# Seven half-width products for 13 of the 16 column pairs of an input projection, with modulation pages, expert rows and scores moved

## The chip, the cores and the metric

One core of one Trainium2 chip runs the whole program in one launch. The metric is the device time in microseconds (us); lower is better. The core has TensorE (PE) for matrix products, VectorE (DVE), ScalarE (ACT), GpSimd (POOL) and SyncE (SP) for the rest and for issuing transfers, and 16 DMA engines that move weights from DRAM into on-chip memory. TensorE writes its results to eight PSUM banks. All data is float32.

## The reference

One inference step of two layers for T = 264 tokens: 256 of a prompt and 8 single new tokens of 8 samples with 256 cached positions each. The model width is 1024.

```python
mod = silu(c) @ w_ada + b_ada                 # six vectors of 1024 for each sequence
h = rms_norm(x, g_mix) * (1 + sc1) + sh1
q, k, v, u, g = split(h @ w_in)               # columns 512 | 512 | 512 | 512 | 2 x 1024
q, k = rms_norm(q), rms_norm(k)               # over heads of 64
o = rms_norm(softmax differences of q k over v)   # samples read cached keys and values
y = pooled windows (2/4/8/16) of u, times w_pool
x += gt1 * ((g0 * (o @ w_branch_a) + g1 * (y @ w_branch_b)) @ w_out)
h2 = rms_norm(x, g_ffn) * (1 + sc2) + sh2
x += gt2 * f(h2)    # layer 0: dense SwiGLU of 2816; layer 1: the best 2 of 8 SwiGLU experts of 3584
```

## The kernel before

Activations are kept transposed: hT holds 1024 features as 8 groups of 128 partitions, with the 264 tokens along the row. Weights come as pages through a ring of 18 slots, which SyncE fills in the order of the list `stream`: before page n it waits until the page that held its slot has been used (`pages_used`). Two column chunks of 128 make one page of 1 MB ("pair").

The input projection makes 32 column chunks. The first 16 of them (pairs 0 to 7: queries, keys, pool input u, values; `Z_ORDER`) are those of the change; 16 more are the gates. Chunk i is the sum of 8 matrix products of 128x128 weights with 264 columns (`z`, L1560); each is two instructions of TensorE. The banks 2 to 5 take turns, VectorE copies the result out (`read_z`, L2308). For each of the 8 query and key chunks ScalarE squares it, TensorE sums the squares (L1651), ScalarE takes the root and VectorE normalises it (`norm_qk`: a reciprocal at L2317, a product at L2321 or L2324). The whole order of instructions on each engine is written out by hand, with semaphores between engines.

In layer 0, four modulation pages (`later_ada`) follow each second chunk: 32 instructions of TensorE at L1470 for the four, and VectorE reads a finished group of 16 with a transposition (`read_mod`, L2091). Sample queries are transposed by TensorE, copied by VectorE (`read_sample_queries`, L2329, behind chunk 10), stored to DRAM (`q_rows`) by GpSimd and loaded back spread over all partitions. `past_scores(b)` then multiplies them with two pages of cached keys of sample b and reduces (L2345, L2348), once for each of the 8 samples; those of samples 0 and 1 stand behind chunks 14 and 15, the others behind the loop, ahead of the prompt's scores (`scores`). TensorE's products for these scores are L1578; the second of them waits for VectorE's copy at L2419, which stands behind sample 6.

The output projection and the feed-forward part of layer 0 already form two chunks at a time from seven half-size products (helper `product`, L1199), with sums of weights on VectorE (L2125 and others) and reads from PSUM with an addition (L2172). A half-size product has 132 columns.

Ahead of layer 0's projection TensorE makes bias rows for the relative positions (L1529); VectorE copies them out (L2300, L2302). Behind layer 1's attention the norm (`norm(3)`: ScalarE copies tokens at L889 and adds the shift at L893) leads to the router and to 16 turns of expert work: gate and up products (L1885) from pages `w_exp_gate` and `w_exp_up`, down products (L1906) from rows of `w_exp_down`, all issued by SyncE (L690, L705). The down rows of a turn are issued in the next turn's loop, between its gate and up pages.

## Time and profile before

| | |
|---|---|
| median of 3 runs | 1605.14 us (1605.09 to 1605.17) |
| profiled execution | 1605.13 us, span 1603.2 us |
| TensorE busy | 1565.8 us (98% of the span) |
| VectorE busy | 541.9 us (34%) |
| ScalarE busy | 181.6 us (11%) |
| GpSimd busy | 69.6 us (4%) |
| DMA | 535.30 MB, mean 334 GB/s |
| layer 0's projection, first 16 chunks | 33.99 to 114.5 us |
| layer 1's projection, first 16 chunks | 484.1 to 545.6 us |
| experts | 702 to 1591 us |

The profile is one execution. Busy times of engines overlap. What an engine waits for is read from semaphores. The span ends with the last instruction; the profiled execution's own time is 1.9 us longer than it.

### The profile page before, as it was taken

The numbers are of one execution on the slowest core, as the hardware profiler recorded it, in microseconds if no ns is written. First come the engines' busy times: TensorE is split into PE (matmuls) and PEld (weight loads), VectorE is DVE, ScalarE is ACT, GpSimd is POOL, SyncE is SP. The second block draws the span as 40 slices with busy tenths as digits, with TensorE's granted clock in tenths as the row PEclk, the third lists the DMA queues.
The fourth block names the chain that finished last, engine by engine and source line by source line (L and its number), as shares of the span: only waits on it lengthen the run. The fifth ranks groups of instructions, "written<-read, shape, count | busy, mean of one in ns | idle before, by whom it ended". The sixth has DMA issues, their size and how long they took to land.

```text
span 1603.2 us, 37188 instructions
## 1 busy us (share of the span) xinstructions
PE 1565.8 (98%) x16734; PEld 1003.9 (63%) x16734; DVE 541.9 (34%) x1182; ACT 181.6 (11%) x486; POOL 69.6 (4%) x118
## 2 busy tenths in 40 slices
PE   7999999999999999999999999999999999999997
PEld 3777898999998878944444444444554555555554
DVE  4368378666554783741101100110011011101132
ACT  2102313111112032131000000000000000000000
POOL 1112400000000110010000000000000000000010
PEclk9999999999999999999999999999999999999999
DMA  9999869666359755569999999999999999999995
GB/s 361 364 386 369 281 219 329 229 223 215 128 174 311 245 165 171 171 237 383 418 418 404 418 418 403 419 418 404 419 402 417 417 398 418 410 406 417 408 378 183
DMA packets 174340, 535.30 MB, mean 334 GB/s; under 512 B 12535, under 2 KB 101413, under 8 KB 161378
## 3 DMA queue, kind: packets, MB, share of 16 engines
q1 hardware_dynamic: 158706, 497.20, 80.9%
q0 software_dynamic: 8768, 28.96, 5.2%
q10 hardware_dynamic: 6704, 6.72, 1.3%
q8 instruction: 134, 2.20, 0.6%
q14 instruction: 28, 0.23, 0.0%
HBM read 517.47 MB, written 15.82 MB: 333 GB/s over the span
## 4 chain that ended last, share of the span: by engine, by line
PE 85%; DMA 11%; DVE 3%; issue 1%; ACT 1%; SPq 0%; DVEq 0%
PE banks L1885 30%; PE banks L1560 14%; PE banks L1199 14%; PE banks L1906 14%; DMA ring<-in_w_exp_up 10%; PE banks L1470 2%; PE banks L1740 2%; PE banks L1231 1%; DVE inv L2504 1%; PE banks L1727 1%; PE banks L1578 1%; DMA ring<-in_w_ada 1%; PE banks L1651 0%; DMA ring<-in_w_exp_down 0%; ACT hT L893 0%
## 5 line engine op out<-in xcount | busy, mean ns | idle before, releaser
L1885 PE MATMUL banks<-ring,area 128*32 128x448 f32 x3072 | 302.6, 539 | 3.3 <-DMA ring<-in_w_exp_up 2.7
L1885 PE MATMUL banks<-ring,xT 128*32 128x448 f32 x3072 | 301.8, 539 | 3.1 <-DMA ring<-in_w_exp_up 3.1
L1560 PE MATMUL banks<-hT,ring 128*128 128x264 f32 x1024 | 239.6, 389 | 3.8 <-ACT hT L893 3.7
L576 DVE TENSOR_TENSOR area<-banks,area 128x448 f32<-128x448 f32 x48 | 46.4, 966 | 576.4 <-ACT area L1157 576.4
L1906 PE MATMUL banks<-area 128*32 128x256 f32 x3840 | 227.4, 379 | 1.4 <-issue 1.1
L1560 PEld LDWEIGHTS banks<-hT,ring 128*128 128x128 f32 x1024 | 193.1, 191 | 39.3 <-issue 6.8
L1885 PEld LDWEIGHTS banks<-ring,area 128*32 128x32 f32 x3072 | 109.8, 110 | 164.5 <-issue 157.4
L1885 PEld LDWEIGHTS banks<-ring,xT 128*32 128x32 f32 x3072 | 111.7, 110 | 160.8 <-issue 151.5
L1906 PEld LDWEIGHTS banks<-area 128*32 128x32 f32 x3840 | 138.8, 110 | 100.6 <-issue 44.2
L1157 ACT ACTIVATE area<-banks 128x448 f32<-128x448 f32 x48 | 26.1, 543 | 779.3 <-PE banks L1885 779.3
L1906 PE MATMUL banks<-ring,area 128*32 128x256 f32 x1536 | 89.4, 379 | 2.0 <-DMA ring<-in_w_exp_down 1.4
L1906 PEld LDWEIGHTS banks<-ring,area 128*32 128x32 f32 x1536 | 55.5, 110 | 39.4 <-issue 13.4
L1199 PE MATMUL banks<-area,ring 128*128 128x132 f32 x480 | 58.4, 277 | 2.3 <-DVE area L2570 1.9
L1199 PEld LDWEIGHTS banks<-area,ring 128*128 128x128 f32 x480 | 56.0, 190 | 3.2 <-DVE area L2570 2.6
L1470 PE MATMUL banks<-ring,cT 128*32 128x256 f32 x768 | 50.1, 397 | 0.8 <-DMA ring<-in_w_ada 0.8
L1199 PE MATMUL banks<-sq,ring 128*128 128x132 f32 x352 | 46.8, 276 | 0.0
L1199 PE MATMUL banks<-area 128*128 128x132 f32 x392 | 45.7, 276 | 0.0
L1199 PEld LDWEIGHTS banks<-area 128*128 128x128 f32 x392 | 44.9, 190 | 0.0
L1199 PE MATMUL banks<-sq,area 128*128 128x132 f32 x352 | 43.3, 276 | 0.1
L1199 PEld LDWEIGHTS banks<-sq,ring 128*128 128x128 f32 x352 | 43.0, 190 | 0.0
L1199 PEld LDWEIGHTS banks<-sq,area 128*128 128x128 f32 x352 | 41.3, 190 | 0.3 <-issue 0.3
L845 POOL DMA_INDIRECT hT<-y_rows,row_of x2 | 2.0, 976 | 813.6 <-ACTq L1165 813.3
(362 smaller groups left out, 1252.7 us busy)
## 6 DMA issues: line engine op xcount, KB each, us to landing
ring<-in_w_exp_gate SPq DMA_DIRECT2D x128, 896.0 KB, 17.6
ring<-in_w_exp_up SPq DMA_DIRECT2D x128, 896.0 KB, 19.7
area<-in_w_exp_down SPq DMA_DIRECT2D x64, 1024.0 KB, 18.1
ring<-in_w_ada SPq DMA_DIRECT2D x96, 512.0 KB, 8.6
ring<-in_w_in SPq DMA_DIRECT2D x32, 1024.0 KB, 13.6
ring<-in_w_exp_down SPq DMA_DIRECT2D x32, 1024.0 KB
...
ring<-in_w_ff_gate SPq DMA_DIRECT2D x11, 1024.0 KB, 6.4
```

The costliest lines, as they stand in the source:

```text
L576: dve.tensor_tensor(F["act_tok"][:, t, :].rearrange("p (i n) -> p n i", i=BODY), bank[3 + t][:, 0:SLICE].rearrange("p (n i) -> p n i", i=B ...
L1157: act.activation(FFN["silu_tok"][:, t, :], bank[t][:, 0:SLICE], ACT.Silu).then_inc(s.silu_e, 1)
L1199: mm = pe.matmul(out, w[c], x[c], start=(first and c == 0), stop=(last and c == n - 1), skip_group_check=True)
L1231: mm = pe.matmul(left(u), w[:, c, 0:P], hT[:, c, 0:HALF], start=(c == 0), stop=(c == 3), skip_group_check=True)
L1470: mm = pe.matmul(bank[b][32 * g:32 * g + 32, half * S:(half + 1) * S].rearrange("p (c n) -> p c n", c=DC), cT[:, r, :], w[:, :, 32 * g:32 ...
L1560: mm = pe.matmul(bank[b][:, 0:T], w[:, c, :], hT[:, c, :], start=(c == 0), stop=(c == DC - 1))
L1578: mm = pe.matmul(bank[4 + 2 * (n % 2) + m][:, 0:w], ATT["q_n"][r, h, i * P:(i + 1) * P], ATT["kT"][r, h, 0:w], start=True, stop=True)
L1727: mm = pe.matmul(bank[2 + j % 2][:, 0:T], branch[j][:, H + c, :], ATT["yT"][:, c, :], start=(c == 0), stop=(c == H - 1))
L1740: mm = pe.matmul(bank[4 + j % 2][:, 0:T], branch[j][:, c, :], oT[:, c, :], start=(c == 0), stop=(c == H - 1))
L1885: mm = pe.matmul(bank[t + 3 * half][32 * g:32 * g + 32, 0:SLICE], tokens[:, t, 32 * r:32 * r + 32], w[half][:, SLICE * g:SLICE * (g + 1)], ...
L1906: mm = pe.matmul(bank[6 + t // 2][32 * q:32 * q + 32, (t % 2) * S:(t % 2 + 1) * S], FFN["actT"][:, m % 2, t, 32 * i:32 * i + 32], wide(at) ...
L2504: step(dve.reciprocal(inv[:, :], root[:, h % 2, :]))
```

## The change

1. **Halved pairs.** For pairs 1 to 7 of layer 0 and 1 to 6 of layer 1 (`Z_HALVED`) the 2x2 blocks of the weights (two chunks by two halves of the 1024 features) and of hT (two halves of features by two halves of the tokens) are combined in seven products of four 128x128 matrix products with 132 columns, in place of eight such products. VectorE makes four sums of weights for each pair (`sum_z`, 128x512 elements each, the last in the page itself) and four sums of hT once for each layer (`sum_h_z`). ScalarE copies products 1, 6 and 5 out of PSUM (`z_one`, `z_two_five`), VectorE adds the others to them (`z11`, `z12`, `z22`) and copies the last (`z21`). Pairs that aren't halved are made as before (`z_whole`), with two banks a pair.
2. **Modulation pages.** Of layer 0's pages 16 to 47, only 16 to 31 stay in its projection. Pages 32 to 39 are streamed between the branch and the output weights and multiplied right ahead of the output projection, 40 to 47 in feed-forward pairs 2 to 5 (`last_ada`). One read of 16 pages becomes two of 8.
3. **Order on VectorE.** `past_scores(0)` and `(1)` follow the projection loop. The sample queries are copied in pair 6, the sample keys in pair 7, modulation in pair 5, the old pool state in pairs 2 and 3.
4. **Bias rows.** ScalarE copies them out, ahead of the projection loop, in place of VectorE.
5. **Unread products.** In layer 0, six products of 256 columns (`WARM`) that nobody reads stand between the last bias row and the first projection product. They need nothing that isn't already there.
6. **Expert rows.** Five down rows of the first turn (`EARLY_ROWS`, 2 + 2 + 1) are issued by ScalarE in `norm(3)`, ahead of its copies of tokens, and SyncE leaves them out later.

```diff
--- before.py
+++ after.py
+WARM = 6
+Z_UNITS = 8
+Z_HALVED = (1, 2, 3, 4, 5, 6, 7), (1, 2, 3, 4, 5, 6)
...
-        STATE_AT = (5, 7)
+        STATE_AT = (2, 3)
...
+        EARLY_ROWS = ((2, 2), (4, 2), (6, 1))
...
-            return range(16 + 2 * (i - 1), min(16 + 2 * (i + 1), 48)) if l == 0 and i % 2 else range(0)
+            return range(16 + 2 * (i - 1), min(16 + 2 * (i + 1), 32)) if l == 0 and i % 2 else range(0)
...
+        def last_ada(i):
+
+            return range(36 + 2 * i, 38 + 2 * i) if 2 <= i <= 5 else range(0)
...
+                    for n in range(32, 40) if (kind, l, j) == ("out", 0, 0) else ():
+                        yield ada_page(0, n)
...
+                    for n in last_ada(j // 2):
+                        yield ada_page(0, n)
...
+        Z_LEFT, Z_RIGHT = (2, 4), (3, 5)
...
-                elif at < RING:
+                else:
                     sp.wait_ge(s.pages_used, STRAIGHT)
-                else:
-                    sp.wait_ge(s.x_new, 3 * DC)
-                    sp.wait_ge(s.pooled, LAYERS)
...
-                            down_rows_in(m - 1, i, n)
+                            if m > 1 or (i, n) not in EARLY_ROWS:
+                                down_rows_in(m - 1, i, n)
...
+                    for i, n_rows in EARLY_ROWS:
+                        at = eslot[2 * DC + i]
+                        act.dma_start(run(at, n_rows), A["w_exp_down"][0, 0, 0:WIDE, :].rearrange(
+                            "(p i) d -> p (i d)", i=BODY)[:, i * D:(i + n_rows) * D]).then_inc(page_in[at], 16)
...
+                def z_one(u):
+                    act.wait_ge(s.product_mm, z_finished(l, 1, u))
+                    act.copy(z_chunk(2 * u)[:, 0:HALF], z_left(u)).then_inc(s.one_kept, 1)
+
+                def z_two_five(u):
+                    act.wait_ge(s.product_mm, z_finished(l, 6, u))
+                    if u >= 2:
+                        act.wait_ge(s.z_out, ZC * l + 2 * (u - 2) + 1)
+                    act.copy(z_kept2[:, u % 2, :], z_left(u)).then_inc(s.two_kept, 1)
+                    act.wait_ge(s.product_mm, z_finished(l, 5, u))
+                    if u - 2 in Z_HALVED[l]:
+                        act.wait_ge(s.c22_read, z_unit(l, u - 2) + 1)
+                    act.copy(z_kept5[:, u % 2, :], z_right(u)).then_inc(s.five_kept, 1)
+
+                if l == 0:
+                    act.wait_ge(s.bias_mm, H + 1)
+                    act.copy(bias_s[:, :], bank[4][0:64, 0:PAST + 1]).then_inc(s.bias_out, 1)
+                    for h in (3, 0, 1, 2):
+                        act.copy(PRO["bias_row"][:, h, :], bank[BIAS_BANK[h]][:, 0:WL]).then_inc(s.bias_out, 1)
+                for u in range(Z_UNITS):
+                    if u in Z_HALVED[l]:
+                        z_one(u)
+                    if 2 <= u < 6:
+                        root_qk(2 * u - 4)
+                        root_qk(2 * u - 3)
+                    if 1 <= u < 5:
+                        square_qk(2 * u - 2)
+                    if u in Z_HALVED[l]:
+                        z_two_five(u)
+                    if 1 <= u < 5:
+                        square_qk(2 * u - 1)
...
+                        for n in last_ada(u // 2):
+                            if n == 40:
+                                pe.wait_ge(s.mod_out, 4)
+                            modulation(0, n, 7)
...
+                if l == 0:
+                    for _ in range(WARM):
+                        pe.matmul(bank[2][:, 0:S], ones, cst[:, 0:S], start=True, stop=True)
...
+                def z_first(u):
+
+                    w, arrived, count = z_page(l, u)
+                    unit[u] = w
+                    pe.wait_ge(arrived, count)
+                    if u >= 2:
+                        pe.wait_ge(s.z_out, ZC * l + 2 * (u - 2) + 2)
+                    if l == 0 and u == 1:
+                        pe.wait_ge(s.bias_out, 2)
+                    for c in range(4):
+                        mm = pe.matmul(z_left(u), w[:, c, 0:P], hT[:, c, 0:HALF], start=(c == 0), stop=(c == 3), skip_group_check=True)
+                    mm.then_inc(s.product_mm, 1)
+
+                def z_second(u):
+
+                    product(z_right(u), [unit[u][:, 4 + c, 0:P] for c in range(4)], [hT[:, 4 + c, 0:HALF] for c in range(4)],
+                            True).then_inc(s.product_mm, 1)
...
+                def z_six_five(u):
+
+                    done = z_unit(l, u)
+                    pe.wait_ge(s.w_summed, z_summed(l, u, 1))
+                    pe.wait_ge(s.one_kept, done + 1)
+                    pe.wait_ge(s.h_summed, 12 * l + 2)
+                    product(z_left(u), z_w(u, 1), z_h(1), False).then_inc(s.product_mm, 1)
+                    pe.wait_ge(s.c11_read, done + 1)
+                    product(z_right(u), z_w(u, 0), z_h(0), True).then_inc(s.product_mm, 1)
+
+                def z_seven_three(u):
+
+                    done = z_unit(l, u)
+                    pe.wait_ge(s.w_summed, z_summed(l, u, 3))
+                    pe.wait_ge(s.two_kept, done + 1)
+                    pe.wait_ge(s.h_summed, 12 * l + 3)
+                    product(z_left(u), [unit[u][:, c, P:2 * P] for c in range(4)], z_h(2), False).then_inc(s.product_mm, 1)
+                    pe.wait_ge(s.five_kept, done + 1)
+                    product(z_right(u), z_w(u, 2), [hT[:, 4 + c, HALF:T] for c in range(4)], False).then_inc(s.product_mm, 1)
+
+                def z_fourth(u):
+
+                    pe.wait_ge(s.c22_read, z_unit(l, u) + 1)
+                    pe.wait_ge(s.h_summed, 12 * l + 4)
+                    product(z_left(u), [unit[u][:, 4 + c, P:2 * P] for c in range(4)], z_h(3), False).then_inc(s.pages_used, 2)
+
+                def z_ada(u):
+
+                    for n in later_ada(l, 2 * u + 1):
+                        modulation(l, n, 0)
...
+                for u in range(Z_UNITS):
+                    if u in Z_HALVED[l]:
+                        z_first(u)
+                        z_second(u)
+                        if u - 1 in Z_HALVED[l]:
+                            z_fourth(u - 1)
+                            z_ada(u - 1)
+                        z_six_five(u)
+                        z_seven_three(u)
+                    else:
+                        if u - 1 in Z_HALVED[l]:
+                            z_fourth(u - 1)
+                            z_ada(u - 1)
+                        z_whole(u)
+                        z_ada(u)
+                    if l == 0 and u in STATE_AT:
+                        turn_state(STATE_AT.index(u))
+                    if 1 <= u < 5:
+                        sum_qk(2 * u - 2)
+                        sum_qk(2 * u - 1)
+                    if u == 5:
+                        turn_sample_queries()
+                    if u == 6:
+                        turn_sample_keys()
+                if Z_UNITS - 1 in Z_HALVED[l]:
+                    z_fourth(Z_UNITS - 1)
+                    z_ada(Z_UNITS - 1)
...
+                if l == 0:
+                    for n in range(32, 40):
+                        modulation(0, n, 7)
                 out_projection(l)
...
+                    if i == 7:
+                        read_mod(0, 7, 40, 47, w_sum[:, 3072:3072 + S], 8).then_inc(s.mod_out, 1)
...
+                def sum_z(u, k):
+
+                    v, arrived, count = z_page(l, u)
+                    if k == 0:
+                        dve.wait_ge(arrived, count)
+                        if u - 2 in Z_HALVED[l]:
+                            dve.wait_ge(s.product_mm, z_finished(l, 3, u - 2))
+                    else:
+                        dve.wait_ge(s.w_summed, z_summed(l, u, (0, 0, 1, 0)[k]))
+                    s1, s2, s4 = (zw_sum[:, u % 2, x, :, :] for x in range(3))
+                    a11, a12, a21, a22 = v[:, 0:4, 0:P], v[:, 4:8, 0:P], v[:, 0:4, P:2 * P], v[:, 4:8, P:2 * P]
+                    if k == 0:
+                        r = dve.tensor_tensor(s1, a21, a22, ALU.add)
+                    elif k == 1:
+                        r = dve.tensor_tensor(s2, s1, a11, ALU.subtract)
+                    elif k == 2:
+                        r = dve.tensor_tensor(s4, a12, s2, ALU.subtract)
+                    else:
+                        r = dve.tensor_tensor(a21, a11, a21, ALU.subtract)
+                    r.then_inc(s.w_summed, 1)
...
+                def z11(u):
+                    c = z_chunk(2 * u)[:, 0:HALF]
+                    dve.wait_ge(s.product_mm, z_finished(l, 2, u))
+                    dve.wait_ge(s.one_kept, z_unit(l, u) + 1)
+                    dve.tensor_tensor(c, z_right(u), c, ALU.add).then_inc(s.c11_read, 1)
+
+                def z12(u):
+                    dve.wait_ge(s.product_mm, z_finished(l, 3, u))
+                    dve.wait_ge(s.two_kept, z_unit(l, u) + 1)
+                    dve.tensor_tensor(z_chunk(2 * u)[:, HALF:T], z_right(u), z_kept2[:, u % 2, :], ALU.add).then_inc(s.z_out, 1)
+
+                def z22(u):
+                    dve.wait_ge(s.product_mm, z_finished(l, 7, u))
+                    dve.wait_ge(s.five_kept, z_unit(l, u) + 1)
+                    dve.tensor_tensor(z_chunk(2 * u + 1)[:, HALF:T], z_left(u), z_kept5[:, u % 2, :], ALU.add).then_inc(s.c22_read, 1)
+
+                def z_read(i):
                     dve.wait_ge(s.pages_used, used_up("z", l, i))
-                    z, b = i % QC, bank[2 + i % 4]
-                    if i // QC != 2:
-                        dst = (ATT["q_raw"], ATT["kT"], None, ATT["vT"])[i // QC]
-                        dve.tensor_copy(dst[:, z, :], b[:, 0:T]).then_inc(s.z_out, 1)
-                    else:
-                        step(dve.tensor_copy(ATT["u_ext"][:, z, BUF:BUF + S], b[:, 0:S]))
-                        dve.tensor_copy(ATT["u_s"][:, z, :], b[:, S:T]).then_inc(s.z_out, 1)
+                    dve.tensor_copy(z_chunk(i), bank[(Z_LEFT, Z_RIGHT)[i % 2][i // 2 % 2]][:, 0:T]).then_inc(s.z_out, 1)
+
+                def z21(u):
+                    dve.wait_ge(s.pages_used, used_up("z", l, 2 * u + 1))
+                    dve.tensor_copy(z_chunk(2 * u + 1)[:, 0:HALF], z_left(u)).then_inc(s.z_out, 1)
...
+                dve.wait_ge(s.h_ready, DC * (2 * l + 1))
+                for u in range(Z_UNITS):
+                    halved, before_halved = u in Z_HALVED[l], u - 1 in Z_HALVED[l]
+                    if before_halved:
+                        z12(u - 1)
+                    if halved and l == 0:
+                        sum_z(u, 0)
+                        sum_z(u, 1)
+                    if halved:
+                        z11(u)
+                    if before_halved:
+                        z21(u - 1)
+                    if halved:
+                        sum_z(u, 2)
+                        sum_z(u, 3)
+                    if u == 0:
+                        sum_h_z(0)
+                        sum_h_z(1)
+                        sum_h_z(2)
+                        sum_h_z(3)
+                    if not halved:
+                        z_read(2 * u)
+                    if 2 <= u < 6:
+                        norm_qk(2 * u - 4)
+                    if u == 6:
+                        read_sample_queries()
+                    if u == 7:
+                        read_sample_keys()
+                    if halved:
+                        z22(u)
+                    if l and u + 1 in Z_HALVED[l]:
+                        sum_z(u + 1, 0)
+                        sum_z(u + 1, 1)
+                    if 2 <= u < 6:
+                        norm_qk(2 * u - 3)
+                    if l == 0 and u in STATE_AT:
+                        read_state(STATE_AT.index(u))
+                    if l == 0 and u == 2:
                         lam_sums()
-                    if 4 <= i < 12:
-                        norm_qk(i - 4)
-                    if i == 10:
-                        read_sample_queries()
-                    if i == 9:
-                        if l:
-                            read_mod(l, 0, 32, 39, spare[:, 0:S], 8).then_inc(s.mod_out, 1)
-                        else:
-                            read_mod(l, 0, 16, 31, spare).then_inc(s.mod_out, 1)
-                        dve.wait_ge(s.mod_out, 4 * l + 2)
-                        step(dve.tensor_scalar(mod[:, 16:24, :], mod[:, 16:24, :], 0.5, None, ALU.mult))
-                    if i == 12:
-                        step(dve.tensor_copy(ATT["u_last"][:, :, 0:BUF], ATT["u_ext"][:, :, S:BUF + S]))
-                        dve.tensor_copy(ATT["u_last"][:, :, BUF:23], ATT["u_s"]).then_inc(s.v_out_u, 1)
-                        read_sample_keys()
-                    if i >= 14:
-                        past_scores(i - 14)
+                    if u == 5:
+                        early_mod()
+                    if u == 6:
+                        last_inputs()
+                    if not halved:
+                        z_read(2 * u + 1)
+                if Z_UNITS - 1 in Z_HALVED[l]:
+                    z12(Z_UNITS - 1)
+                    z21(Z_UNITS - 1)
+                past_scores(0)
+                past_scores(1)
...
-                if l == 0:
-                    read_mod(l, 1, 32, 47, spare).then_inc(s.mod_out, 1)
...
+                if l == 0:
+                    read_mod(0, 7, 32, 39, ATT["prob"].rearrange("p a b -> p (a b)")[:, 0:S], 8).then_inc(s.mod_out, 1)
```

## Rows read from the trace of the kernel before

**Rows 1.** Page, the chain that ended last, by engine (share of the span)
```profile
PE 85%; DMA 11%; DVE 3%; issue 1%; ACT 1%; SPq 0%; DVEq 0%
```

**Rows 2.** Windows: busy (count) of PE, PEld, DVE, ACT, POOL; clock, DMA, GB/s
```profile
684.60:694.40 9.80, 7.40 (x81) 4.04 (x79) 7.06 (x29) 8.92 (x19) 0.00 (x0) 1.00 0.01 3
800.00:1100.00 300.00, 300.00 (x3993) 129.48 (x3984) 26.81 (x42) 10.73 (x21) 0.00 (x0) 1.00 1.02 412
```

**Rows 3.** Groups of VectorE instructions by form: busy us, mean ns | idle before
```profile
L2317 DVE RECIPROCAL inv<-root 128x264 f32<-128x264 f32 x16 | 28.7, 1796 | 0.0
...
L2125 DVE TENSOR_TENSOR area<-ring 128x512 f32<-128x512 f32 x22 | 14.1, 682 | 0.0
...
L2172 DVE TENSOR_TENSOR area<-banks,area 128x132 f32<-128x132 f32 x26 | 7.7, 295 | 47.8 <-PE banks L1199 46.9 <-ACT area L1050 0.9
...
L2324 DVE SCALAR_TENSOR_TENSOR area<-area,vecT,inv 128x264 f32<-128x264 f32 x8 | 3.9, 494 | 0.3
...
L2091 DVE STREAM_TRANSPOSE area<-banks 128x512 f32<-128x512 f32 x4 | 2.8, 709 | 0.0
```

**Rows 4.** The chain in order of time: start us, us, what
```profile
49.10 3.56 PE banks L1560 x16
...
399.07 62.56 PE banks L1199 x556
```

**Rows 5.** Timeline of layer 0's projection: start us, us, engine, instruction
```profile
33.99 9.04 PE L1560 MATMUL banks<-hT,ring 128*128 128x264 f32 x32 [2.04 <-ACT hT L893]
...
39.51 0.43 DVE L2308 COPY area<-banks 128x264 f32<-128x264 f32 x1 [1.25 <-PE banks L1560]
...
47.57 0.51 SPq L666 DMA_DIRECT2D ring<-in_w_in  x1
...
112.50 1.93 PE L1470 MATMUL banks<-ring,cT 128*32 128x256 f32 x32
```

**Rows 6.** DMA issues, windows 47:52, 93:105, 528:545: KB, us to landing
```profile
ring<-in_w_in SPq DMA_DIRECT2D x1, 1024.0 KB, 14.4
...
q_rows<-area POOLq DMA_DIRECT2D x1, 16.0 KB, 4.9
...
area<-q_rows POOLq DMA_DIRECT2D x1, 1024.0 KB, 7.8
...
q_rows<-area POOLq DMA_DIRECT2D x1, 16.0 KB, 1.8
```

**Rows 7.** Windows, TensorE alone: length, busy, granted clock, DMA share, GB/s
```profile
36.00:37.00 1.00, 1.00 (x4) 0.50 1.06 365
```

**Rows 8.** Timeline of sample queries and score products, layers 0 and 1
```profile
136.21 0.67 DVE L2419 COPY area<-banks 23x512 f32<-23x512 f32 x1
...
138.79 0.70 PE L1578 MATMUL banks<-area 64*128 64x256 f32 x4
...
529.96 0.67 DVE L2329 COPY area<-banks 8x512 f32<-8x512 f32 x1
...
542.58 0.68 DVE L2345 TENSOR_TENSOR area<-area 128x512 f32<-128x512 f32 x1
...
566.19 0.67 DVE L2419 COPY area<-banks 23x512 f32<-23x512 f32 x1
...
569.80 0.70 PE L1578 MATMUL banks<-area 64*128 64x256 f32 x4
```

**Rows 9.** Waits of TensorE, 690 to 1603: us, times, longest
```profile
PE banks L1885 <- DMA ring<-in_w_exp_up: 5.8, 8, 1.8
PE banks L1906 <- DMA ring<-in_w_exp_down: 1.4, 1, 1.4
```

**Rows 10.** DMA issues of 800 to 900, then of 1100 to 1200 us
```profile
ring<-in_w_exp_up SPq DMA_DIRECT2D x15, 896.0 KB, 15.6
...
ring<-in_w_exp_up SPq DMA_DIRECT2D x15, 896.0 KB, 20.4
```

**Rows 11.** Timeline of ScalarE in the last norm
```profile
686.05 3.30 ACT L893 ACTIVATE hT<-hT,mod 128x256 f32<-128x256 f32 x8 [0.27 <-DVE hT L2085]
```

269 lines of the change are left out of this document (150 added, 119 removed).

## The prediction

> **What bounds the kernel now.** The page comes first: the chain that ended last is 85% TensorE and 11% DMA [rows 1]. So an edit pays if it takes time from TensorE, or from the DMA share. The windows then show where that share lies. In the expert stage TensorE is busy in all of 300 us while the 16 DMA engines are busy too, at 412 GB/s [rows 2]. There both are full. Before about 690 us DMA is lighter and TensorE alone sets the pace, so the reader should keep two budgets: TensorE ahead of 690 us, DMA behind it. The third view is VectorE's groups [rows 3], because the change hands VectorE work in the stage that it edits.
>
> The base: the profiled execution took 1605.13 us around its 1603.2 us span, and the median of the runs is 1605.14, so differences of the span count one for one.
>
> **1. Halving, TensorE alone.** A whole pair of column chunks is 2 x 16 instructions, 2 x 3.56 = 7.12 us [rows 4]. An instruction of a half-width product takes 62.56/556 = 0.1125 us, a product of eight 0.90 us [rows 4]. Seven products are 6.30 us, so each halved pair saves 0.82 us: 7 pairs 5.7 us in layer 0, 6 pairs 4.9 us in layer 1. This is 10.7 us if nobody is late.
>
> **2. Halving, VectorE.** Somebody is late. A halved pair costs VectorE four sums of 512 columns, three 132-column additions from PSUM and a 132-column copy, beside two head normalisations in pairs 2 to 5 [rows 3]. In the sums' group 22 x 0.682 is 15.0 us and busy is 14.1: independent neighbours overlap 0.08 us, while one that waits for its predecessor starts some 0.03 us after it. Sums 0.72 + 3 x 0.61 = 2.55; reads 4 x (0.295 - 0.08) = 0.84; normalisations, reciprocal and product, 2 x (1.80 + 0.03 + 0.49 - 0.08) = 4.48; together 7.87 us. TensorE wants 6.30 plus two sums of squares, each of two instructions of 3.56/16 = 0.22 us: 7.18. Before, a pair took 7.12 + 0.88 = 8.00. So with all buffers doubled VectorE sets the pace in the middle of layer 1: pairs 1 and 2 keep 0.82 each, pairs 3 to 5 keep about 0.13 each, and pair 6 comes behind a VectorE that has also read modulation (a transposition and two small operations, some 0.95) and normalised the last key: I work out 2.1 us of waiting for product 5's reader. Sum -1.6 - 0.4 + 1.3 = -0.7, and with hand-overs (0.3 us from a product to its reader) -0.6 instead of -4.9. In layer 0 pairs 1 to 3 carry modulation on TensorE (1.93 a group [rows 5]), which covers VectorE; behind pair 5, whose modulation read is twice as wide (0.71 for the transposition [rows 3], some 1.3 in all), pair 6 waits 2.6 us, and the last product of pair 7 another 0.6.
>
> **3. Pages in layer 0.** Up to page 31 the stream is unchanged, and pair 3, issued at 47.57, lands 14.4 us later, at 62.0 [rows 5, 6]. TensorE would now be ready at 60, so it waits 2.0, with 0.3 at pair 2. Bounds: 0 (the queue hurries) to 3.
>
> **4. Unread products.** After the last bias row TensorE idles for 2.04 us, until 33.99 [rows 5], and from 35 to 38 us the granted clock is 0.50, that is 1.2 GHz [rows 7]. The first pair takes 9.04 us instead of 7.12, and its first chunk, read at 39.51, ends at about 39.3 [rows 5]. Six products of 256 columns are 12 x 0.22 x 256/264 = 2.6 us: the first projection starts at 34.5 instead of 34.0, but at 2.4 GHz its first chunk ends at 38.1 instead of 39.3. Gain 1.2 (bounds 0 and 1.6). The bias evictions (2.4 us) leave VectorE for ScalarE, which idles there.
>
> **5. Sixteen modulation pages.** Four are 1.93 us [rows 5], 1.95 with the gap: 7.8 us go out of layer 0's projection, 3.9 come back ahead of the output projection and 3.9 in feed-forward pairs 2 to 5. TensorE is full at all three places, and two modulation reads of some 0.7 on VectorE replace one of 1.0, so the move itself is 0. Its cover matters: these pages also hid VectorE. So layer 0's projection ends 7.8 (moved) + 1.2 (clock) + 5.7 (halving) - 2.3 (pages) - 3.2 (VectorE) = 9.2 earlier; with the smaller gaps 8.9.
>
> **6. What is late next.** Scores against old keys (two multiplications of 0.68 us [rows 8] and two reductions of the same size, 2.9 us a sample row with their turns, eight rows) stood for two rows inside the projection loop; now all follow it. They need the sample queries, which go through DRAM: in layer 1 copied at 529.96, stored in 1.8 us, spread in 7.8, and with copy and issues 10.9 us after the copy began they are there; they are first used at 542.58 [rows 6, 8]. The copy moves behind pair 6's sums, by my working to 534.5, and the first score to 545.5 (+2.9). TensorE's second score product waits for what follows seven rows of this: VectorE ended at 566.19 + 0.67 = 566.86 and TensorE came at 569.80 [rows 8]. That 2.9 us of slack is used up: VectorE is ready at 566.86 + 2.9 + 0.4 (two scores now queue behind the copies), with 0.2 of hand-over at 570.4; TensorE comes at 569.80 - 0.6 = 569.2 and waits 1.2, and for the sample weights, later still, I allow 0.5. Layer 1's attention ends -0.6 + 1.2 + 0.5 = **1.1 us later**. In layer 0 the slack is 138.79 - (136.21 + 0.67) = 1.9 [rows 8]. The DMA queues are emptier there without the 16 pages, so I take layer 1's latencies; then the same waits are 1.2 and 0.5, and the stage ends 8.9 - 1.7 = 7.2 earlier. Repaying 7.8: **0.6 later**.
>
> **7. Five down rows early.** Before, the first turn's down rows are issued behind the second turn's gate and up pages, while the DMA engines move 3 GB/s from 684.6 to 694.4 us [rows 2]. TensorE then waits 5.8 us for gate/up pages and 1.4 for down rows [rows 9], and the time from issue to landing of an up page grows from 15.6 to 20.4 us between the windows 800 to 900 and 1100 to 1200 us [rows 10]: DMA falls behind 4.8 us in 300, about 1.6 in 100. Five rows are 2.62 MB, at 412 GB/s 6.4 us of lead, taken in the idle time. That covers 6.4 of 7.2. Bounds 0 and 7.2. ScalarE issues them: three issues, an estimated 0.45 us each by SyncE's issue of a page (0.51 [rows 5]), ahead of its copies, which left only 0.27 us of idle before the scaling activations [rows 11]. Behind those stand the router and the turned rows: 1.35 - 0.27 = 1.1 us later. Net **-5.3**.
>
> On this the Trainium skill ("DMA: Bandwidth & Descriptors", Issuing engines are not separate DMA queues) says that issuing from another engine adds no bandwidth, since all use the same 16 engines. The trace agrees that the late part has none to give (412 GB/s, share 1.02 [rows 2]); by that rule the rows pay only because of the 9.8 us ahead in which the engines idle, and with these engines busy the item would be 0 + 1.1 and the total 1607.9. The same page's Bandwidth section puts the limit of loads from HBM at about 358 GB/s; the trace has 412, and the measurement decides.
>
> **Sum.** +0.6 + 1.1 - 5.3 = -3.6: 1605.1 - 3.6 = **1601.5**.
>
> **The rivals.**
> - VectorE keeps pace: reads, sums and normalisations overlap by more than my 0.08. For it: before, VectorE was never what the head sums waited for, with 4.5 of these 7.9 us a pair. Against: 7.87 against 7.18 leaves no room. Items 2 and 6 then give 1.8 us in layer 0 and 3.6 in layer 1, and without the page wait 2.3 more: 1601.5 - 5.4 = 1596.1, at most 1593.8. Chance 0.17.
> - The early rows give nothing: DMA was limited by the slots' turn, not by a lead. Then item 7 is +1.1: 1607.9. For it: SyncE waits mostly for TensorE. Against: latency grows steadily. Chance 0.08.
> - The chain of old keys becomes the bound (slower). Place: TensorE's second score product. Price: layer 0's store of the queries took 4.9 us where layer 1's took 1.8 [rows 6]; at 4.9 in both the first score comes 3.1 us later, and with half as much again for key pages that land late the loss is 4.6 us a layer, 9.2 in both: 1610.7. It decides once the first score starts more than about 4 us after the projection ends. In one layer alone 1606.1. For it: the queues are fuller with pages that arrive ahead of need. Against: 16 pages fewer are in them. Chance 0.15.
> - TensorE's clock: waits over 2 us (pair 6, pair 3) are like the idle of [rows 5, 7] and may be followed by 3 us at 1.2 GHz, 1.5 us each. One or two of them more than forecast give 1603.0 to 1604.5, no change. Chance 0.15.
> - The forecast as worked out: 0.45, its own range 1599 to 1604.
>
> **Numbers.** About 0.2% (3.2 us) is what a measurement of this kernel can tell from no change. Below 1601.9 lie over half of the forecast and the first rival: 0.50. Above 1608.3 lie most of the two-layer key case and the edge of the early-row case: 0.13. The rest, 0.37, is no change. The range 1595.5 to 1607.5 leaves out the two-layer key case, most of the early-row one and the extreme of the first.
>
> **What would show it.** Right: in layer 1, TensorE waits for VectorE before products 5 and 7 of pairs 3 to 6, pair pitch 7.9; product pitch 0.90; a TensorE wait of 1 to 2 us before the second score product; no half clock at 35 us; up-page landing near 9 us at 800 us and waits for up pages under 1.5 us in all. Wrong: pair pitch 7.2 in layer 1, a first score later than 548 or waits for up pages still at 1180 us.

## The result, and the profile after

The changed kernel took 1610.53 us (median of 11 runs, 1607.75 to 1614.29) against 1605.14 us of the kernel before: ratio 1.0034, 95% interval 1.0026 to 1.0042 (the kernel before ran 11 times beside it, 1603.89 to 1607.63). It is 5.4 us **slower**; 1601.5 us and a gain were forecast. The profiled execution took 1612.15 us around a span of 1610.5 us, so its span is 7.3 us longer than before's, and the ledgers below add up to that.

First where the chain of the last end lies now, by engine (page); it answers to [rows 1]:

```profile
PE 84%; DMA 8%; DVE 5%; issue 1%; ACT 1%; SPq 0%; ACTq 0%; DVEq 0%; POOLq 0%
```

DMA has given up 3 points of share, as the early rows meant it to (in the changed kernel without them it is 14%), and VectorE has gained 2.

Then TensorE's timeline in layer 0 (start us, us, instruction, idle time ahead and its cause); it answers to [rows 5] and to the layer 0 part of [rows 8]. L1772 is a whole pair, L1717 and L1279 are half-width products, L1555 modulation, L1657 scores:

```profile
32.62 2.86 PE L1621 MATMUL banks<-cst 128*128 128x256 f32 x12
35.32 7.28 PE L1772 MATMUL banks<-hT,ring 128*128 128x264 f32 x32
...
54.02 2.13 PE L1717 MATMUL banks<-hT,ring 128*128 128x132 f32 x8 [3.01 <-DMA ring<-in_w_in]
55.94 1.97 PE L1279 MATMUL banks<-hT,ring 128*128 128x132 f32 x8
57.70 1.97 PE L1279 MATMUL banks<-area,ring 128*128 128x132 f32 x8
59.60 2.22 PE L1555 MATMUL banks<-ring,cT 128*32 128x256 f32 x32
...
67.67 1.06 PE L1279 MATMUL banks<-hT,ring 128*128 128x132 f32 x8
68.57 1.06 PE L1279 MATMUL banks<-area,ring 128*128 128x132 f32 x8
69.56 1.93 PE L1555 MATMUL banks<-ring,cT 128*32 128x256 f32 x32
...
97.68 3.73 PE L1279 MATMUL banks<-area 128*128 128x132 f32 x16 [2.33 <-DVE area L2494]
101.25 1.06 PE L1279 MATMUL banks<-area,ring 128*128 128x132 f32 x8
...
138.51 1.03 PE L1657 MATMUL banks<-area 64*128 64x256 f32 x4 [2.68 <-DVE area L2640]
139.47 5.14 PE L1639 MATMUL banks<-hT,ring 128*128 128x264 f32 x16
```

The reader should see two things. There are three new waits: for the page of pair 2 (3.01 us), for a sum of weights at pair 6 (2.33) and for VectorE's copy ahead of the second score product (2.68). And behind each of them the same work takes about twice its time: a product starts 1.8 to 1.9 us before the next one at 54 to 60 us, and 0.90 at 67.67 to 68.57. The windows say why (length, TensorE's busy time, granted clock, DMA share, GB/s):

```profile
54.00:60.00 6.00, 5.98 (x28) 0.50 1.05 383
...
98.00:101.00 3.00, 3.00 (x15) 0.50 1.08 344
...
697.00:702.00 5.00, 4.40 (x31) 0.66 0.95 369
```

The granted clock is 0.50, which is 1.2 GHz, right behind the waits. Three products and four pages take 61.75 - 54.02 = 7.73 us instead of 3 x 0.90 + 1.87 = 4.57; the two products at 97.68 take 3.57 instead of 1.80; score product and gate chunk 6.03 instead of the 4.39 that they take in layer 1 (584.27 - 579.88). That is 3.2 + 1.8 + 1.6 = **6.6 us lost to the clock**, about as much as the whole result. The profile before holds one such stretch too, worth 1.9 us (9.04 for the first pair in place of 7.12). The last window shows a fourth in the changed kernel, behind a wait of 2.29 us ahead of the router, where the profile before has 1.00; it comes back under the early rows.

Layer 1, the same view (it answers to the layer 1 part of [rows 8]):

```profile
516.19 2.09 PE L1279 MATMUL banks<-area 128*128 128x132 f32 x16
518.52 1.17 PE L1279 MATMUL banks<-area,ring 128*128 128x132 f32 x8 [0.23 <-DVE ring L2498]
...
521.31 1.06 PE L1717 MATMUL banks<-hT,ring 128*128 128x132 f32 x8
...
529.13 1.06 PE L1717 MATMUL banks<-hT,ring 128*128 128x132 f32 x8
...
541.59 1.17 PE L1279 MATMUL banks<-area 128*128 128x132 f32 x8 [1.32 <-DVE area L2513]
...
579.88 0.70 PE L1657 MATMUL banks<-area 64*128 64x256 f32 x4 [2.24 <-DVE area L2640]
```

The first six rows are pairs 3 to 6 (the wait of 1.32 us is at pair 6), the last is the second score product. From the first product of pair 4 (521.31) to that of pair 5 (529.13) it is 7.82 us: VectorE's pace, forecast as 7.87. VectorE's groups by form (busy us, mean ns), which answer to [rows 3], have the sizes that the sum used:

```profile
L2538 DVE RECIPROCAL inv<-root 128x264 f32<-128x264 f32 x16 | 28.7, 1794 | 0.0
...
L2492 DVE TENSOR_TENSOR area<-ring 128x512 f32<-128x512 f32 x13 | 8.9, 682 | 3.5 <-DMA ring<-in_w_in 3.5
...
L2513 DVE TENSOR_TENSOR area<-banks,area 128x132 f32<-128x132 f32 x13 | 3.8, 290 | 8.4 <-PE banks L1279 8.4
```

VectorE's own timeline shows why the second score product waits: the query copy, the first score against old keys, a later one that waits for its key page, and the copy that the product needs:

```profile
542.85 0.67 DVE L2550 COPY area<-banks 8x512 f32<-8x512 f32 x1
...
553.97 0.68 DVE L2566 TENSOR_TENSOR area<-area 128x512 f32<-128x512 f32 x1
...
561.48 0.69 DVE L2566 TENSOR_TENSOR area<-area 128x512 f32<-128x512 f32 x1 [1.48 <-DMA area<-in_cache_k]
...
579.15 0.67 DVE L2640 COPY area<-banks 23x512 f32<-23x512 f32 x1
```

Behind the attention: the experts' waits (us, times, longest), answering to [rows 9], and the landing of up pages between 800 and 900, then between 1100 and 1200 us, answering to [rows 10]:

```profile
PE banks L2064 <- DMA ring<-in_w_exp_up: 3.1, 5, 1.2
...
PE banks L2085 <- DMA ring<-in_w_exp_down: 0.3, 1, 0.3
```

```profile
ring<-in_w_exp_up SPq DMA_DIRECT2D x15, 896.0 KB, 10.8
...
ring<-in_w_exp_up SPq DMA_DIRECT2D x15, 896.0 KB, 16.5
```

Landing is 4.8 and 3.9 us sooner than before, and 3.8 of 7.2 us of waits are gone. The price stands in ScalarE's timeline, answering to [rows 11]: three issues, and the copies that start behind them.

```profile
692.74 1.31 ACTq L936 DMA_DIRECT2D area<-in_w_exp_down  x3
694.09 2.05 ACT L943 COPY area<-banks 128x512 f32<-128x512 f32 x4 [0.88 <-PE banks L1941]
```

The stages of the two profiled executions, from TensorE's timelines (first projection product, first branch product, first expert product, first of the last products at 1592.18 and 1599.40):

| stage | before | after | difference | forecast |
|---|---|---|---|---|
| start of layer 0's projection | 33.99 | 35.32 | +1.33 | +0.5 |
| layer 0, projection to branch | 157.67 | 157.69 | +0.02 | |
| layer 0's branch to layer 1's projection | 292.45 | 299.69 | +7.24 | +7.8 |
| layer 0 in all, with the start | | | **+8.59** | **+0.6** |
| layer 1, projection to branch | 138.56 | 140.36 | +1.80 | +1.1 |
| branch to experts | 79.46 | 80.59 | +1.13 | +1.1 |
| experts | 890.05 | 885.75 | -4.30 | -6.4 |
| sum | | | +7.22 | -3.6 |

All but 2.8 us of the 10.8 us between forecast and profile lie in layer 0.

### The profile page after: what moved, and what is told of

Same layout as the page of the kernel before. It is cut to its first block, busy times and chain, and to the rows that moved or that the text cites. A ratio compares the mean times of both kernels' runs of the same rounds, so it can differ in the third digit from the quotient of the medians.

```text
span 1610.5 us, 38041 instructions
## 1 busy us (share of the span) xinstructions
PE 1566.0 (97%) x17058; PEld 987.2 (61%) x17058; DVE 577.3 (36%) x1257; ACT 191.9 (12%) x530; POOL 69.6 (4%) x118
## 3 DMA queue, kind: packets, MB, share of 16 engines
q8 instruction: 137, 2.24, 0.6%
## 4 chain that ended last, share of the span: by engine, by line
PE 84%; DMA 8%; DVE 5%; issue 1%; ACT 1%; SPq 0%; ACTq 0%; DVEq 0%; POOLq 0%
PE banks L2064 34%; PE banks L1279 17%; PE banks L2085 16%; PE banks L1639 5%; DMA ring<-in_w_exp_up 4%; PE banks L1555 2%; DMA area<-in_cache_k 2%; PE banks L1916 2%; PE banks L1311 1%; DMA ring<-in_w_in 1%; PE banks L1772 1%; DVE inv L2764 1%; PE banks L1903 1%; DVE area L2566 1%; DVE inv L2538 1%
## 5 line engine op out<-in xcount | busy, mean ns | idle before, releaser
L2064 PEld LDWEIGHTS banks<-ring,area 128*32 128x32 f32 x3072 | 101.0, 110 | 171.5 <-issue 162.7
L2085 PEld LDWEIGHTS banks<-area 128*32 128x32 f32 x3840 | 129.2, 110 | 110.2 <-issue 46.3
L1639 PE MATMUL banks<-hT,ring 128*128 128x264 f32 x512 | 120.8, 390 | 0.0
L1639 PEld LDWEIGHTS banks<-hT,ring 128*128 128x128 f32 x512 | 96.4, 192 | 16.9 <-issue 1.4
L1279 PE MATMUL banks<-area,ring 128*128 128x132 f32 x688 | 87.8, 279 | 3.7 <-DVE area L2830 1.9
L1279 PEld LDWEIGHTS banks<-area,ring 128*128 128x128 f32 x688 | 82.3, 192 | 5.7 <-DVE area L2830 2.6
L1279 PE MATMUL banks<-area 128*128 128x132 f32 x600 | 74.0, 281 | 3.7 <-DVE area L2494 2.3
L2085 PEld LDWEIGHTS banks<-ring,area 128*32 128x32 f32 x1536 | 51.7, 110 | 42.2 <-issue 14.3
L1279 PEld LDWEIGHTS banks<-area 128*128 128x128 f32 x600 | 71.2, 194 | 5.5 <-DVE area L2494 2.5
L1555 PE MATMUL banks<-ring,cT 128*32 128x256 f32 x768 | 50.3, 403 | 0.7 <-DMA ring<-in_w_ada 0.4
L1279 PE MATMUL banks<-hT,ring 128*128 128x132 f32 x344 | 46.4, 280 | 0.7 <-ACT hT L947 0.7
L1279 PE MATMUL banks<-sq,ring 128*128 128x132 f32 x352 | 46.8, 276 | 0.0
L1279 PE MATMUL banks<-hT,area 128*128 128x132 f32 x344 | 45.7, 276 | 0.0
L1279 PE MATMUL banks<-sq,area 128*128 128x132 f32 x352 | 43.3, 276 | 0.1
L1279 PEld LDWEIGHTS banks<-hT,ring 128*128 128x128 f32 x344 | 42.8, 193 | 0.9 <-ACT hT L947 0.9
```

The costliest lines, as they stand in the source:

```text
L1279: mm = pe.matmul(out, w[c], x[c], start=(first and c == 0), stop=(last and c == n - 1), skip_group_check=True)
L1555: mm = pe.matmul(bank[b][32 * g:32 * g + 32, half * S:(half + 1) * S].rearrange("p (c n) -> p c n", c=DC), cT[:, r, :], w[:, :, 32 * g:32 ...
L1639: mm = pe.matmul(bank[b][:, 0:T], w[:, c, :], hT[:, c, :], start=(c == 0), stop=(c == DC - 1))
L2064: mm = pe.matmul(bank[t + 3 * half][32 * g:32 * g + 32, 0:SLICE], tokens[:, t, 32 * r:32 * r + 32], w[half][:, SLICE * g:SLICE * (g + 1)], ...
L2085: mm = pe.matmul(bank[6 + t // 2][32 * q:32 * q + 32, (t % 2) * S:(t % 2 + 1) * S], FFN["actT"][:, m % 2, t, 32 * i:32 * i + 32], wide(at) ...
```

## The experiments

Two theories came out of the profile. **Waits and clock**: layer 0's new waits, and the 1.2 GHz that follows them, cost what the halving saves. **VectorE's chain**: the chain sums, then old-key scores, then copies sets the end of the attention, and what TensorE wins or loses ahead of it doesn't count. A third was open for each part alone: that it did what the forecast had said. All ratios are to the kernel before, run on the same chip, with 95% intervals. Its median there was 1602.67 us for the early rows alone, the unread products alone, those in two waits and the two copies; 1605.32 for no unread products, layer 1 whole and the two runs with pages back; 1602.93 for the others. So ratios can be compared across groups, and microseconds only within one.

**Early rows alone** (the kernel before, with the change's sixth part only):

```diff
+                    for i, n_rows in EARLY_ROWS:
+                        at = eslot[2 * DC + i]
+                        act.dma_start(run(at, n_rows), ...).then_inc(page_in[at], 16)
...
-                            down_rows_in(m - 1, i, n)
+                            if m > 1 or (i, n) not in EARLY_ROWS:
+                                down_rows_in(m - 1, i, n)
```

> The kernel before with only the five early down rows. Theory: the profile of the changed kernel has the experts' start 1.1 us later against the branch stage and gives 4.3 us back until the end, so this alone should give about -3.2 us, 1602; TensorE's waits for up pages fall from 5.8 to about 3. Rival (the rows gain nothing, DMA is limited by the slots' turn): 1606, waits as before. My forecast's own figure was -5.3, 1599.8.

Measured: 1599.42 us, ratio 0.9979 (0.9969 to 0.9988), -3.3 us: the theory's figure, not the forecast's 5.3. TensorE's waits for up pages stayed at 5.8 us in its profile, against the expectation of 3; up pages landed after 11.0 us at 800 to 900 us. So landing improves as in the changed kernel, but the sum of waits of one execution is no good measure of it.

**Unread products alone** (the kernel before with the six products):

```diff
+                if l == 0:
+                    for _ in range(6):
+                        pe.matmul(bank[2][:, 0:S], ones, cst[:, 0:S], start=True, stop=True)
```

> The kernel before with only the six unread products. Theory of the forecast: -1.2 us, no half clock at 35 us. What the changed kernel's profile shows is 1.3 us later at the first product and 0.4 us earlier at the end of the first pair, so -0.4 us is the other figure. Rival: the half clock comes all the same, or comes later: +0.5 to +1.3 us.

Measured: 1603.12 us, ratio 1.0003 (0.9994 to 1.0012). The timeline of this run and that of the run above, where nothing stands in the gap:

```profile
33.01 2.86 PE L1536 MATMUL banks<-cst 128*128 128x256 f32 x12
35.71 7.28 PE L1563 MATMUL banks<-hT,ring 128*128 128x264 f32 x32
```

```profile
34.87 7.36 PE L1565 MATMUL banks<-hT,ring 128*128 128x264 f32 x32 [2.03 <-ACT hT L898]
...
55.05 3.80 PE L1565 MATMUL banks<-hT,ring 128*128 128x264 f32 x16 [0.68 <-DMA ring<-in_w_in]
...
115.61 3.80 PE L1565 MATMUL banks<-hT,ring 128*128 128x264 f32 x16 [1.06 <-DMA ring<-in_w_in]
```

After the same idle time (2.03 us against the 2.04 of [rows 5]) the first pair took 7.36 us here and 9.04 in the profile before. **The half clock follows a wait in some executions and not in others.** Where it doesn't, the products only push the start back, by 0.8 us. And where it doesn't, TensorE waits for pages later on: in the run above for pair 2's (0.68 us) and for the first gate's (1.06), in this one for the latter,

```profile
115.47 3.80 PE L1563 MATMUL banks<-hT,ring 128*128 128x264 f32 x16 [1.08 <-DMA ring<-in_w_in]
```

and in the profile before, with the half clock, for neither. From the projection's start to layer 0's branch it is 157.67 us in the profile before and 157.91 in the run above: the 1.7 us that the first pair took less were waited for again. In this run it is 156.92. With the products every one of the 11 executions showed a mean granted clock of 0.999; the 32 of the kernel before beside it 0.996 to 0.999.

**No unread products** (the changed kernel, `WARM = 0`):

> The changed kernel without the six unread products. Theory from the run of these products alone (+0.5 us): the first projection product comes 0.8 us sooner where the clock stays at 2.4 GHz, and page arrival at pair 2 and VectorE behind it take that up: ratio to before 1.0025 to 1.0035, as the changed kernel's 1.0034. Rival (the forecast's term): 1.2 us slower than the changed kernel, 1.0041.

Measured: 1608.74 us, ratio 1.0022 (1.0013 to 1.0031), so not slower than the changed kernel. In its profile the first pair ran into the half clock (9.97 us) and TensorE waited only 0.3 us for pair 2's page, in place of 3.0. In the nine profiles in which TensorE waits for that page as a halved pair's it goes on between 53.65 and 54.17 us, whatever the first pair took. The page's landing is a fixed point near 54 us; what the clock gives ahead of it is waited for again. How far executions differ is seen here too: this one, the fastest of 12 (1605.71 us), had no half clock behind the page nor at the score product, and layer 0 from projection to branch took 152.3 us, against 157.7 in the changed kernel's profile.

**Unread products in two waits** (the changed kernel; seven ahead of pair 2, five ahead of pair 6's sixth product, in a free bank):

```diff
+                        if l == 0 and u == 2:
+                            pe.wait_ge(s.bias_out, H + 1)
+                            fill(7)
                         z_first(u)
...
+                        if l == 0 and u == 6:
+                            pe.wait_ge(s.state_out, LAYERS)
+                            fill(5)
                         z_six_five(u)
```

> The changed kernel with unread products (256 columns, into the free bank 1) placed in two of layer 0's waits: seven ahead of pair 2's first product and five ahead of pair 6's sixth. The waits themselves stay. Theory: TensorE's clock at 1.2 GHz behind these two waits cost 3.1 and 1.8 us; with full clock 1610.5 - 4.9 = 1605.6. Rival: VectorE sets the time behind them anyway, so what TensorE gains it waits for again: 1608 to 1610.5.

Measured: 1606.88 us, ratio 1.0030 (1.0021 to 1.0039). The clock did what was expected: 0.50 at neither place, and pair 2 is on time.

```profile
50.02 3.19 PE L1709 MATMUL banks<-cst 128*128 128x256 f32 x14
54.05 1.17 PE L1721 MATMUL banks<-hT,ring 128*128 128x132 f32 x8 [0.84 <-DMA ring<-in_w_in]
55.06 1.06 PE L1279 MATMUL banks<-hT,ring 128*128 128x132 f32 x8
```

But the wait ahead of the second score product grew from 2.7 to 3.7 us (waits of TensorE, 34 to 200 us), and half clock followed it (1.22 us for the four instructions that take 0.70 at full clock):

```profile
PE banks L1657 <- DVE area L2650: 3.7, 1, 3.7
```

By the medians the rival came closer: repairing the clock in these two places gives 0.6 us where 4.9 were expected, and the intervals overlap. That VectorE's chain takes it up is shown for a part. In this profile layer 0 from projection to branch is still 1.8 us shorter than in the changed kernel's (155.85 against 157.69), after a wait that is 1.0 longer. The run without early rows (below) has the same code in this stage as the changed kernel, and full clock at pair 6 without any filling; there the wait is as long, and half clock follows it as well:

```profile
136.32 1.22 PE L1657 MATMUL banks<-area 64*128 64x256 f32 x4 [3.60 <-DVE area L2640]
```

**Two copies on ScalarE** (the changed kernel; the copies at L2638 and L2640 leave VectorE's place behind sample 6):

```diff
+                    if g == 4:
+                        if l:
+                            act.wait_ge(s.pooled, l)
+                        act.wait_ge(s.vs_mm, 2 * l + 1)
+                        act.copy(ATT["vs_tok"], bank[0][0:NS, :]).then_inc(s.vs_out, 1)
+                        act.wait_ge(s.vs_mm, 2 * l + 2)
+                        act.copy(ATT["u_tok"], bank[6][0:23, :]).then_inc(s.vs_out, 1)
...
-                past_scores(2); read_v(0); past_scores(3); read_v(1); past_scores(4); past_scores(5); past_scores(6); read_new()
+                past_scores(2); read_v(0); past_scores(3); read_v(1); past_scores(4); past_scores(5); past_scores(6)
```

> The changed kernel with the two copies of new values and pool inputs (8 and 23 rows of 512) on ScalarE, behind the third gate's result, in place of VectorE behind sample 6. Theory: the second score product waits for nothing else; both waits (2.7 and 2.2 us) and the half clock behind the first (1.8 us) go: 1610.5 - 6.7 = 1603.8. Rival: VectorE's chain of old keys is late as a whole and the next product that needs it (the raw scores' turning, the third score) waits instead: 1608 to 1610.5.

Measured: 1602.64 us, ratio 1.0003 (0.9994 to 1.0012), 5 us less than the changed kernel's ratio gives. The second score product no longer waits; the third does, for less:

```profile
132.94 0.70 PE L1664 MATMUL banks<-area 64*128 64x256 f32 x4
133.58 3.83 PE L1646 MATMUL banks<-hT,ring 128*128 128x264 f32 x16
138.74 0.49 PE L1664 MATMUL banks<-area 64*128 64x128 f32 x4 [1.34 <-DVE area L2622]
```

From the projection's start to the branch it is 154.14 us in layer 0 and 138.15 in layer 1, against 157.69 and 140.36. Both theories have their share: the chain made the wait, and the clock made it dear.

**Both of these** (unread products in the waits, copies on ScalarE):

> The changed kernel with both the unread products in the waits at pairs 2 and 6 and the two copies on ScalarE. Theory: with the second score product's wait gone, TensorE can keep what full clock gives it (up to 4.9 us where the half clock falls in both places, less where it doesn't): ratio between 0.9975 and 0.9995, against 1.0003 with the copies alone. Rival (VectorE's chain takes it up at the next place): 1.0003.

Measured: 1601.92 us, ratio 0.9995 (0.9986 to 1.0004): some 1.3 us below the copies alone, with intervals that overlap. Its mean granted clock is 0.9981 over 11 runs, against 0.9967 with the copies alone and 0.995 in the 11 runs of the changed kernel.

**Layer 1 whole** (no pair of layer 1 halved):

> The changed kernel with all eight pairs of layer 1 whole (layer 0 as changed, order on VectorE as changed). Theory: layer 1's six halved pairs keep 0.8 us of 4.9 ahead of the gates, and the wait of the second score product hangs on VectorE's chain that starts at the loop's end, so it stays near 2 us: 0.8 us slower than the changed kernel, ratio 1.0039. Rival (VectorE keeps pace and the halving is worth 4.9): 1.0065.

Measured: 1611.93 us, ratio 1.0037 (1.0025 to 1.0048). Six halved pairs, 4.9 us on TensorE, are worth 0.5 us (the intervals overlap); the wait of layer 1's second score product stays, at 2.0 us. Layer 1 from projection to branch takes 140.95 us whole, and halved 140.36 in the changed kernel's profile and 139.5 to 139.8 in four others with the same layer 1, so the halving is worth 0.6 to 1.4 us by that stage.

**Pages back** (the 16 modulation pages again in layer 0's projection; the streaming and the products at their later places are left out, and VectorE reads the second group of 16 as one, behind the loop):

```diff
-            return range(16 + 2 * (i - 1), min(16 + 2 * (i + 1), 32)) if l == 0 and i % 2 else range(0)
+            return range(16 + 2 * (i - 1), min(16 + 2 * (i + 1), 48)) if l == 0 and i % 2 else range(0)
```

> The changed kernel with the 16 modulation pages back in layer 0's projection. Theory: on TensorE they are worth nothing wherever they stand (7.8 us), but there they cover VectorE's sums and scores: the waits at pairs 6 and 7 (2.8 us) and at the second score product (2.7) and the half clocks behind them go, some 5.5 to 7 us, ratio 1.0034 - 0.0037 = 0.9997 or less. Rival (the cover is worth nothing, the page wait at pair 2 and the queue are what costs): ratio stays 1.003, and layer 0's waits for weights grow.

Measured: 1606.05 us, ratio 1.0007 (0.9997 to 1.0017), 4.3 us less than the changed kernel. The waits at pairs 6 and 7 are gone, that for pair 2's page is not, and, against the theory, the one at the second score product stays and grows (waits of TensorE, 34 to 250 us):

```profile
PE banks L1655 <- DVE area L2635: 3.4, 1, 3.4
PE banks L1715 <- DMA ring<-in_w_in: 3.1, 1, 3.1
PE banks L1642 <- DVE mod L2269: 1.1, 1, 1.1
```

VectorE's timeline names a cause that the theory left out. It waits for the sample queries on their way through DRAM, ahead of its first old-key score, which in the changed kernel's profile it did not:

```profile
115.40 0.69 DVE L2561 TENSOR_TENSOR area<-area 128x512 f32<-128x512 f32 x1 [2.41 <-DMA area<-q_rows]
```

Projection to branch is 161.39 us with the pages and 157.69 without: 7.24 us of work moved out gave only 3.7 there.

**Pages back and copies on ScalarE:**

> Both: the pages back in layer 0's projection and the two copies on ScalarE. Theory: layer 0 gives nothing more than with the pages back alone, as no wait is left there; layer 1's wait (2.2 us) goes: ratio 0.9997 - 0.0014 = 0.9983. Rival (waits add up independently): 0.9966.

Measured: 1604.25 us, ratio 0.9990 (0.9981 to 0.9999): 2.7 us below the pages back alone, where the theory has 2.2 and the rival 5. The interval leaves out the rival's 0.9966. Both start from a pages-back figure that came out 1.6 us too low.

**No early rows** (the changed kernel with `EARLY_ROWS = ()`):

> The changed kernel without the five early rows. Theory: their effect adds to the rest, as it was 0.21% alone: ratio 1.0034 + 0.0021 = 1.0055. Rival (they only shift the experts' waits in the changed kernel, which starts 10 us later with other gaps): 1.0034.

Measured: 1609.62 us, ratio 1.0042 (1.0029 to 1.0056; five runs). The interval holds both figures, so this time doesn't decide. Its up pages landed after 15.6 and 20.4 us in the two windows, as in [rows 10], which puts the shorter landing down to the rows. From the first expert product to the last products its profile takes 886.8 us, and 882.6 to 883.7 in the three runs of the same group that keep the rows: the gain of the stage is there in the changed kernel too.

**No pair halved** and **seven pairs halved** (order of the changed kernel, pages back, copies on ScalarE, no unread products, early rows kept; with none it is `Z_HALVED = (), ()`, with seven as shown):

```diff
-Z_HALVED = (1, 2, 3, 4, 5, 6, 7), (1, 2, 3, 4, 5, 6)
+Z_HALVED = (3, 4, 5, 6, 7), (1, 2)
```

> No pair halved in either layer: the changed kernel's order on VectorE, pages back in layer 0's projection, the two copies on ScalarE, no unread products, early rows kept. Theory: as the kernel before with the early rows alone, ratio 0.9979, with up to 1 us of waits for scores that start only at the loop's end: 0.9979 to 0.9985. Rival (the moved old-key scores cost several us by themselves): above 0.999.

> The same with only those pairs halved that have room: 3 to 7 of layer 0, where the page is there and modulation pages cover VectorE, and 1 and 2 of layer 1. Theory: seven pairs keep nearly the whole 0.82 us each, 5.7 us below the kernel without halved pairs: ratio 0.9979 - 0.0036 = 0.9945 to 0.9955. Rival (VectorE's chain to the scores takes it up again): 0.9975 to 0.9985.

Measured: 1601.57 us, ratio 0.9993 (0.9984 to 1.0002) with none, 1600.67, 0.9984 (0.9975 to 0.9993) with seven. In both the rival came closer. The first is above the early rows alone by 2.2 us, so the order with all old-key scores behind the loop seems to cost something by itself (waits of 1.1 us at the scores and 0.9 at the sample weights in layer 0), although the intervals overlap. The second is 1.5 us lower where seven pairs should save 5.7. In its timeline TensorE waits for pair 6's page (in the run with pages back and copies on ScalarE it waited 0.47 us there) and 1.18 us for the first gate's:

```profile
93.44 1.17 PE L1722 MATMUL banks<-hT,ring 128*128 128x132 f32 x8 [1.97 <-DMA ring<-in_w_in]
```

In layer 1 its two halved pairs gave 0.6 us of 1.6 (137.99 against 138.56 from projection to branch), with a wait of 0.73 us at the sample weights.

No version with halved pairs came out below the kernel before with the early rows alone (0.9979; the interval of the seven pairs overlaps with its own).

## Why the prediction was wrong, point by point

**What bounds the kernel: wrong for layer 0.** The prediction put "DMA is lighter" on everything ahead of 690 us, from a view of the expert stage alone. A window of the kernel before that it didn't use (length, TensorE's busy time, clock, DMA share, GB/s) says otherwise, and the DMA column of [rows 7] already had 1.06:

```profile
60.00:80.00 20.00, 20.00 (x142) 1.00 1.04 385
```

In layer 0's projection the DMA engines were as full as in the expert stage, by share (1.04 against 1.02; 385 and 412 GB/s). TensorE could be made faster there only as far as pages were ahead. That is shown by the page waits at pair 2 and, with seven pairs, at pair 6, by the page waits of the early rows alone and the unread products alone (1.7 and 1.1 us with no pair halved), and by the run without unread products, where half clock and page wait took each other's place.

**Halving on TensorE and on VectorE (steps 1 and 2): right.** Product pitch 0.90 us; pair pitch in layer 1 7.82 against 7.87; layer 1's projection ends 0.8 us sooner against 0.6 (the transposition behind the first gate chunk comes at 556.91 - 492.70 = 64.21 us behind the first product, before at 549.14 - 484.11 = 65.03). The rival in which VectorE keeps pace is refuted.

**Pages in layer 0 (step 3): right in size, wrong in place.** 2.3 us were forecast, 3.0 measured, but all of it at pair 2, whose page, issued at 35.7, takes 18.3 us, not at pair 3.

**Unread products (step 4): a gain that isn't there.** -1.2 us were forecast, alone they gave +0.5 (-1.0 to +1.9). Two reasons are shown: the half clock at 35 us comes only in some executions, and what it costs is hidden by page waits, at pair 2 in the changed kernel and at pair 2 and the first gate in the kernel before. The start came at 35.3, not 34.5, as the bias rows ended 0.7 us later in this execution.

**Moved pages (step 5): the cover mattered more than was allowed.** They cost 7.24 us where they went (7.8 forecast) and gave back 3.7 where they left. Net 3.5 us, shown by the run with the pages back (4.3 by the medians).

**What is late next (step 6): the right mechanism, too small in layer 0.** The forecast had this product wait 1.2 us in either layer; it waited 2.68 and 2.24. Other profiles give 2.4 and 3.6 us with the same layer 0, 1.6 in the one without unread products, and 1.4, 1.4, 1.4 and 1.7 with the same layer 1. So in layer 1 the forecast was near (+1.0 to +1.2 us for the stage in those four, forecast +1.1), and in layer 0 it was not. The first score came when forecast (553.97; 545.5 plus the 8.6 us by which layer 1 is late). What was left out is that VectorE's waits for key pages ahead of the copy grow: from 1.9 to 2.7 us in layer 0 and from 0.6 to 2.9 in layer 1. That the wait hangs on two copies in VectorE's queue, and not on the scores themselves, the run with the copies on ScalarE shows.

**The waits of layer 0 (steps 2, 3 and 6, and the fourth rival, the clock): the step that failed.** The forecast had layer 0 end 0.6 us later; in the profile it ended 8.6 later. Its sum had waits of 2.0, 2.6 and 1.2 us there, entered each at its own length and put the clock behind them at nothing; that stood only as a rival, at 0.15, "one or two of them more than forecast", 1.5 us each. In the profile three stretches at 1.2 GHz came and cost 6.6 us, and the wait at the second score product was 2.68 in place of 1.2. What the runs show of the two is this. With that product's copies on ScalarE, which takes away the wait and the clock behind it, 5.0 us of the changed kernel's loss go. With two gaps filled and the wait left, 0.6 us go by the ratios; with both, 6.3. Over the runs the clock stands beside the time only in part: 0.995 on average in the changed kernel against 0.998 before, 0.9967 and 0.9981 in the two runs that are 5 to 6 us faster, but 0.996 with the two gaps filled, at nearly the changed kernel's time. How much of the 5.4 us is clock on average stays open.

**Early rows (step 7): right sign, two thirds of the size.** -5.3 were forecast, -3.3 measured alone. The cost, 1.1, came out at 1.13 in the profile, but partly by luck: the wait behind ScalarE grew by only 0.5 us (1.79 to 2.29), and the rest is the half clock behind it (697 to 702 us). In five profiles with early rows and full clock there, branch to experts takes 79.95 to 79.97 us, 0.5 more than before. The gain was taken as the whole lead in bytes, 6.4 us; landing improved by 4.8 falling to 3.9, and the stage by 4.3. The rival in which they give nothing is refuted.

**The sum.** In layer 0 the profile is 8.0 us worse than forecast: 6.6 clock, 0.7 more for the page, 1.5 more at the score product, 0.8 more for the start and first pair; less 0.3 for VectorE's waits at pairs 6 and 7 (2.85 for 3.2), 0.5 for a wait at the sample weights that didn't come and 0.6 for the moved pages. That makes 8.2. Layer 1 adds 0.7, the experts 2.1. The rival "the chain of old keys becomes the bound" named the place and the sign of the outcome, 1606.1 for one layer and 1610.7 for both, at a chance of 0.15. Its price rested on sample queries that come late from DRAM, and VectorE waited for none in this profile; only the later key pages did come. That its 1610.7 is the measured time is luck.

## What to carry to other kernels

Before a stage is made shorter on one engine, read the DMA share of that very stage: a full queue turns the gain into a page wait. Price a new wait on TensorE with what may stand behind it, the time at 1.2 GHz, and treat that as a draw that comes in some executions; in the changed kernel's profile a wait of 2.7 us cost 4.3. And where TensorE waits for a copy in a busy engine's queue, move the copy to an idle engine before anything else: here moving two copies gave 5 us, and six halved pairs 0.5.
